# A trunk layer with seven-product feed-forward units: the snapshot of the seventh product and the high half of T1,T2 change places on ScalarE

## What is computed

```python
def swiglu(h, w_gate, w_up, w_down):
    return (jax.nn.silu(h @ w_gate) * (h @ w_up)) @ w_down
...
x = x + 0.5 * swiglu(rms_norm(x, ffn1_norm[l]), ffn1_gate[l], ffn1_up[l], ffn1_down[l])
x = x + hybrid_mixer(rms_norm(x, mix_norm[l]), ...)
x = x + 0.5 * swiglu(rms_norm(x, ffn2_norm[l]), ffn2_gate[l], ffn2_up[l], ffn2_down[l])
```

## Time and profile before

| | us |
|---|---|
| median of 3 runs | 956.42 (956.31 to 956.98) |
| the profiled execution | 956.84, of it span 955.0 |
| TensorE busy with matmuls | 943.2 |
| VectorE busy | 677.2 |
| ScalarE busy | 435.0 |
| GpSimd busy | 358.0 |

### The profile page before, as it was taken

One profiled execution on the slowest core, in us unless ns is written; L12 is line 12 of the kernel. 1 busy time (PEld: TensorE's weight loads), 2 busy tenths in 40 slices (PEclk: granted clock), 3 DMA queues, 4 the chain that ended last, 5 costly groups with the idle time before them and its releaser, 6 DMA issues. The chain is left out here.

```text
span 955.0 us, 16547 instructions
## 1 busy us (share of the span) xinstructions
PE 943.2 (99%) x6290; PEld 843.6 (88%) x6290; DVE 677.2 (71%) x956; ACT 435.0 (46%) x686; POOL 358.0 (37%) x241
## 2 busy tenths in 40 slices
PE   9999999999999999999999999999999999999997
PEld 8889999999888889777899788889999999988887
DVE  6699999997643375677578964379999999833444
ACT  7564455555522223654534333544555545632331
POOL 0777776763010135110100014387767677000001
PEclk9999999999999999999999999999999999999999
DMA  6332324232232325222212122233232332222232
GB/s 210 120 102 90 130 88 132 88 121 71 99 100 100 102 76 175 75 74 78 76 52 68 45 89 91 86 132 111 89 129 91 115 104 91 86 100 77 100 100 89
DMA packets 31104, 94.27 MB, mean 99 GB/s; under 512 B 4464, under 2 KB 7712, under 8 KB 31056
## 3 DMA queue, kind: packets, MB, share of 16 engines
q1 hardware_dynamic: 29120, 90.28, 28.7%
q0 software_dynamic: 1648, 3.07, 1.2%
q10 hardware_dynamic: 288, 0.26, 0.1%
HBM read 90.38 MB, written 2.42 MB: 97 GB/s over the span
## 5 line engine op out<-in xcount | busy, mean ns | idle before, releaser
L1481 DVE TENSOR_TENSOR w_lo<-raw,w_hi 128x1024 fp32r<-128x1024 f32 (+2 forms) x128 | 193.8, 1514 | 147.1 <-ACT w_hi L1103 147.0
L1103 ACT ACTIVATE w_hi<-raw 128x1024 fp32r<-128x1024 f32 (+2 forms) x128 | 131.4, 1026 | 194.4 <-PE ps L570 194.3
L568 PE MATMUL ps<-xg_hi,w_hi 128*128 128x256 f32 (+1 forms) x528 | 178.2, 338 | 0.8 <-DVE w_lo L1481 0.6
L570 PE MATMUL ps<-xg_hi,w_lo 128*128 128x256 f32 (+1 forms) x528 | 175.0, 331 | 0.0
L569 PE MATMUL ps<-xg_lo,w_hi 128*128 128x256 f32 (+1 forms) x528 | 174.8, 331 | 0.0
L568 PE MATMUL ps<-s_hi,sum_hi 128*128 128x256 f32 x576 | 160.2, 278 | 2.5 <-ACT snap L1198 2.3
L569 PE MATMUL ps<-s_lo,sum_hi 128*128 128x256 f32 x576 | 159.4, 277 | 0.0
L570 PE MATMUL ps<-s_hi,sum_lo 128*128 128x256 f32 x576 | 159.2, 276 | 0.0
L569 PE MATMUL ps<-h_lo,w_hi 128*128 128x512 f32 x330 | 128.4, 389 | 0.0
L568 PEld LDWEIGHTS ps<-xg_hi,w_hi 128*128 128x128 f32 x528 | 99.9, 189 | 19.1 <-issue 8.2
L568 PEld LDWEIGHTS ps<-s_hi,sum_hi 128*128 128x128 f32 x576 | 108.4, 188 | 3.6 <-issue 3.4
(11 more groups left out here) (255 smaller groups left out, 1888.9 us busy)
## 6 DMA issues: line engine op xcount, KB each, us to landing
raw<-up_w SPq DMA_DIRECT2D x50, 512.0 KB, 4.0
raw<-down_w SPq DMA_DIRECT2D x38, 512.0 KB, 3.2
raw_u<-up_w SPq DMA_DIRECT2D x36, 512.0 KB, 3.2
raw<-t_w SPq DMA_DIRECT2D x15, 512.0 KB, 3.3
raw<-out_w SPq DMA_DIRECT2D x8, 512.0 KB, 3.3
raw<-nat_w SPq DMA_DIRECT2D x4, 576.0 KB, 3.8
x<-xT SPq DMA_DIRECT2D x8, 256.0 KB, 4.8
out<-x SPq DMA_DIRECT2D x8, 256.0 KB, 2.2
```

Source lines behind the costliest of these rows:

```text
L568: pe.matmul(out_ap, a[0], b[0], start=first, stop=False, skip_group_check=resumed)
L570: return pe.matmul(out_ap, a[1], b[0], start=False, stop=last, skip_group_check=resumed)
L1103: act.activation(dst, raw[:, slot(s), 0:w], ACT.Copy).then_inc(hi_ready, 1)
L1481: dve.tensor_tensor(lo, raw[:, slot(s), 0:w], hi, ALU.subtract).then_inc(lo_ready, 1)
```

## The change

In `unit` on ScalarE, ga of the next unit is no longer the last instruction of a unit. Each unit now begins with snapshot 2 of the unit before, then its own ga, then gb. The numbers that ga waits for are the same, and it is made for the same units; ga of unit 0 stays where it was, ahead of the units.

```diff
--- before.py
+++ after.py
@@ -1209,6 +1209,7 @@
                     s = up0 + 2 * PLAIN + b
                     if prev:
                         take(2, *prev, A_BANK, m7_done, c22_done)
+                        ga(i, b)
                         gb(i, b)
                     if prev and isinstance(i, int) and v == FAST - 1:
                         split_hi(s + 2 * i + 1)
@@ -1222,8 +1223,6 @@
                     act.activation(sum_hi[:, GC, :], raw_u[:, b, :].rearrange("p (a c) -> p a c", a=2), ACT.Copy)\
                         .then_inc(gc_hi, 1)
                     take(1, i, b, A_BANK, m6_done, c12_done)
-                    if not (isinstance(i, int) and v == FAST - 1):
-                        ga(*((i, 1) if b == 0 else (i + 1, 0)))
 
                 for m in range(PLAIN):
                     pair(m)
```

## The result

| | before | after |
|---|---|---|
| median of 6 runs, us | 956.50 (956.31 to 956.98) | 959.75 (959.46 to 960.66) |
| the profiled execution, us | 956.84 | 960.66 |
| its span, us | 955.0 | 958.9 |

The changed kernel is slower, by a ratio of 1.0034 with a 95% interval of 1.0024 to 1.0045: 3.3 us on 956.5. The profiled execution of the changed kernel is the slowest of its six, so what has to be found in its profile is 3.9 us of span and not 3.3. One later execution of the kernel before took 1886.39 us, about twice its usual time, and counts in no ratio here.

A forecast was written before the change was run, and what follows sets the result against it. TensorE, busy 943.2 of 955.0 us, was taken as the bound, with the VectorE-ScalarE chain nearly as long. Steady stalls of +3.2 us and -0.3 us at the second stage's start gave +2.9 on 956.42: 959.3 us, range 956.0 to 961.2.

The forecast's parts named there:

- The low half at S + 1.38: VectorE's low half of T1,T2 in each steady unit starts at S + 1.38, not S + 0.90: 0.48 us later.
- S: Start of ScalarE's snapshot of a unit's seventh product on TensorE, the point from which the chain's times are counted.
- The 6.67 us behind it and the 0.22 us joint: Low half to end of the sixth product's snapshot unchanged, 6.67 us; then 0.22 us until TensorE can start the seventh product.
- Stalls of 0.16 and 0.08 us in 28 units, +3.2 us: TensorE stalls 0.16 us after ScalarE's loop turns, 0.08 us elsewhere, 14 units in each of two stages: +3.2 us.
- The way they would show: Profile after: TensorE waiting for the snapshot some 30 times, not 4, for 0.1 us or less each.
- -0.3 us at the second stage's opening: Snapshot freed from behind GpSimd's sums: VectorE's low half ends at 666.21, not 666.54, -0.3 us.
- Nothing at the first stage's opening: No gain counted at the other waits: a GpSimd sum or other VectorE work ends there where it did.
- The order on the shared ports holds: GpSimd's first sum still starts ahead of VectorE's slab split, by about 0.3 us; the split stays 2.3 us long.
- The rival: VectorE's slab split starts ahead of GpSimd's sum and ends 1.1 us earlier: 956.1 to 956.4 us, 10 in 100.
- The rival that ended on the faster side: Freed snapshot removes all four TensorE waits at the starts, steady units keep their slack: 953.2 us, 4 in 100.
- The forecast's range of +1.0 to +4.6 us: Span given to the forecast itself, 957.4 to 961.0 us, said to follow its terms' bounds; 68 in 100.

The follow-up runs named there:

- t3_first: The changed kernel, but ScalarE makes the high half of T3 before that of T1,T2; 974.33 us, ratio 1.0187 to the kernel before.
- the two halves: The kernel before with the high half of T1,T2 moved only in even units (958.35 us) or only in odd units (959.65 us).
- opening_moved: The kernel before with the instruction moved only for units 1 and 2 of each stage; 956.47 us, ratio 1.0002.
- odd_moved: The kernel before with the instruction moved only in the odd units, second of a pair; 959.65 us, ratio 1.0029.
- after_best: The changed kernel, GpSimd's first sum waiting for the gate slab's low half from unit 2, VectorE's mixer start-up around the first stage's last unit; 954.95 us.
- opening_start_late: The kernel before, instruction moved only in units 1 and 2, VectorE's mixer start-up work around the first stage's last unit; 954.97 us, ratio 0.9985.
- after_sums_wait: The changed kernel with GpSimd's first sum also waiting for the gate slab's low half from unit 2 on; 955.07 us, ratio 0.9985.
- even_moved: The kernel before with the instruction moved only in the even units, first of a pair; 958.35 us, ratio 1.0018.
- start_late: The kernel before with VectorE's start-up work for the mixer around the first stage's last unit, not between units 1 and 2; 955.24 us, ratio 0.9985.
- before_sums_wait: The kernel before with GpSimd's first sum also waiting for the gate slab's low half from unit 2 on; 959.43 us, ratio 1.0029.
- again: The changed kernel run once more, unaltered, against the kernel before; 960.14 us, ratio 1.0039.

## Why the prediction was right

The prediction was 959.3 us and slower; measured 959.75, which is +3.25 on the median of six where I had +2.9 on the median of three.

- *The low half at S + 1.38.* Measured S + 1.36 and 1.37 in all steady units. Right; t3_first and the two halves show that it is this start that carries the cost. The idle time that I expected before it is only 0.1 us: VectorE itself comes later, with c22 at S + 0.81 and not S + 0.56, since the gating of the unit before ends at 134.35 + 1.77 = 136.12.
- *The 6.67 us behind it and the 0.22 us joint.* The snapshot ends at S + 8.03 to 8.05 (forecast 8.05), the load 0.11 us behind it. Right.
- *Stalls of 0.16 and 0.08 us in 28 units, +3.2 us.* +3.4 and +3.3 us in the two profiles. Right, and with the larger part in the units behind the loop turn: +0.15 for even units alone, +0.11 for odd ones. In detail two small errors offset each other: a pair costs 0.22 to 0.31 us and not 0.24, and 26 units stall and not 28 (see the shared ports below).
- *The way they would show.* Wrong: I expected some 30 waits in the profile, there are four. A stall of a tenth of a microsecond is swallowed by the recorded end of the matmul before; it is seen in the spacing of the weight loads, the longer first matmul, S to S, and the number of matmuls in a window.
- *-0.3 us at the second stage's opening.* Right, -0.3 in both profiles, and for the reason given.
- *Nothing at the first stage's opening.* Off by +1.1 us and +0.5 us in the two profiles of this kernel, on account of a slab that lands 1.3 us late; in opening_moved, where it was not late, this opening took the same time as before within 0.1 us. From issue to first sum it took 4.9 to 5.1 us in both of these profiles and in those of odd_moved, after_best and opening_start_late. It was not late in opening_moved (3.33), t3_first (3.32) and after_sums_wait (3.88, with the sum started by its new wait), in all of which unit 1 is moved as well, and in none of the four with unit 1 unmoved: before, even_moved, start_late and before_sums_wait. So the move alone does not bring it about. Five of eight against none of four hints that the move makes it likelier, but that is **not settled**. That it is what makes the runs of these kernels spread is not shown.
- *The order on the shared ports holds.* Right: 12 of 12 splits in the first stage's middle take the long form, GpSimd 0.3 us ahead. Of the 56 splits in units 2 to 15 of the two profiles four took 1.22 us, with GpSimd behind, and just those units did not stall. In unit 3 of the second stage of `again` the split starts at 688.61, and S to S is 695.19 - 685.50 = 9.69 us, as in the kernel before, with the low half at S + 1.36. The rival would have given this in every unit, as after_sums_wait does.

The rival that ended on the faster side stood on the four waits in the openings. They were worth something, as start_late shows (1.4 us), but not by this change. The forecast's range of +1.0 to +4.6 us does not come out of the bounds of its terms, which run from -1.5 to +6.3; no working stands for it, so that the time fell inside it says less than the terms do.

## What to carry to other kernels

When TensorE is full and two other engines are nearly so, write down the chain that goes from one TensorE event through them to the next, and set it against TensorE's own period: an engine that is idle half of the time can still lie on it, and here some 0.47 us later meant 0.13 us in each of 26 units, because the first 0.33 to 0.41 us was slack, while the next 0.52 us went through whole. An order in an engine's list is good or bad by which of its waits is the late one: the same swap cost 3.3 us with early sums and won 4.4 us with late ones. Measure small stalls by the distance of like events over many rounds, or by the number of matmuls in a window, and not by the list of waits.

## What the runs showed that I had not expected

- Two instructions that exclude each other on VectorE and GpSimd need about the same time together in either order (from the start of the first to the end of the second 2.43 us at 136.49 and 2.35 us at 214.54), yet the order counts: ahead of GpSimd's sum the slab split of the steady units takes 1.22 us instead of 2.32, and the chain that TensorE waits for is 1.1 us shorter there.
- The load of 512 KB for the second slab of unit 2 in the first stage took 3.2 to 3.6 us from its issue to its first user in the profiles of some kernels and 4.9 to 5.1 in others. It was issued at the same place of the program and 4.9 us behind the start of the stage's first sixth-product snapshot in all of them, with the next load 1.2 us behind it where this was looked up (before, changed and opening_moved).
